# Latent attention: rotary halves of the queries exchanged between partitions by transfers, in place of products with a second copy of the columns

## What is computed

```python
def apply_rope(x, ang):                       # x: 64 features of a head
    x1, x2 = jnp.split(x, 2, axis=-1)         # two halves of 32
    c, s = jnp.cos(ang), jnp.sin(ang)
    return jnp.concatenate([x1 * c - x2 * s, x2 * c + x1 * s], axis=-1)

def mla_mixer(hn, kv, positions, w_q_a, q_g, w_q_b, w_o):
    k_nope, k_pe, v = kv                      # k_pe: one rotary key for all heads
    cq = rmsnorm(hn @ w_q_a, q_g)             # 384 latent features
    q = (cq @ w_q_b).reshape(B, S, 8, 128 + 64)
    q_nope, q_pe = q[..., :128], apply_rope(q[..., 128:], angles)
    o = attention(q_nope, q_pe, k_nope, k_pe, v)   # masked softmax of the sum of both products
    return o.reshape(B, S, 1024) @ w_o
```

## Time and profile before

| | us |
|---|---|
| median of 3 runs | 977.38 |
| lowest, highest | 976.89, 977.48 |
| the profiled execution | 976.76 |
| its span, first to last instruction | 974.8 |
| TensorE busy in it | 958.3 (98%) |
| VectorE, ScalarE, GpSimd busy | 663.8 (68%), 500.6 (51%), 33.2 (3%) |

### The profile page before, as it was taken

One profiled execution on the slowest core, in us unless ns is written; L12 is line 12 of the kernel. 1 busy time (PEld: TensorE's weight loads), 2 busy tenths in 40 slices (PEclk: granted clock), 3 DMA queues, 4 the chain that ended last, 5 costly groups with the idle time before them and its releaser, 6 DMA issues.

```text
span 974.8 us, 15160 instructions
## 1 busy us (share of the span) xinstructions
PE 958.3 (98%) x6065; PEld 862.4 (88%) x6065; DVE 663.8 (68%) x838; ACT 500.6 (51%) x664; POOL 33.2 (3%) x48
## 2 busy tenths in 40 slices
PE   8999999999999998999999999999999999999997
PEld 8999998999999996899998888888899888888885
DVE  5866757687677777677658765666767676655564
ACT  5855663664554557443346434444655464443442
POOL 2000001200000000000000000001010000000000
PEclk9999999999999999999999999999999999999999
DMA  9942212566565544655555565655464446565641
GB/s 294 262 130 87 87 65 88 167 208 210 174 212 172 194 153 140 208 170 173 173 173 186 183 207 179 209 172 195 124 158 173 128 134 235 173 201 187 203 142 44
DMA packets 124799, 165.05 MB, mean 169 GB/s; under 512 B 20910, under 2 KB 103275, under 8 KB 124619
## 3 DMA queue, kind: packets, MB, share of 16 engines
q1 hardware_dynamic: 123131, 159.31, 50.6%
q0 software_dynamic: 1312, 4.68, 1.6%
q10 hardware_dynamic: 304, 0.33, 0.1%
HBM read 163.26 MB, written 1.05 MB: 169 GB/s over the span
## 4 chain that ended last, share of the span: by engine, by line
PE 95%; DVE 2%; ACT 1%; issue 1%; DMA 0%; POOL 0%; POOLq 0%; DVEq 0%; ACTq 0%
PE ps L276 23%; PE ps L278 22%; PE ps L277 22%; PE ps L900 11%; PE ps L897 6%; PE ps L2036 2%; PE ps L1415 2%; PE ps L1436 1%; PE ps L2031 1%; PE ps L1299 1%; PE ps L538 1%; DVE w_lo L239 0%; PE ps L1425 0%; PE ps L2165 0%; DMA X<-in_x_dram 0%
## 5 line engine op out<-in xcount | busy, mean ns | idle before, releaser
L239 DVE TENSOR_TENSOR w_lo<-raw,w_hi 128x2048 fp32r<-128x2048 f32 x147 | 334.3, 2276 | 135.8 <-ACT w_hi L225 135.8
L225 ACT ACTIVATE w_hi<-raw 128x2048 fp32r<-128x2048 f32 x147 | 279.8, 1905 | 141.0 <-PE ps L278 139.5
L276 PE MATMUL ps<-hT,w_hi 128*128 128x256 f32 x712 | 203.7, 286 | 1.4 <-DVE hT L497 0.9
L277 PE MATMUL ps<-hT,w_lo 128*128 128x256 f32 x712 | 201.4, 283 | 0.0
L278 PE MATMUL ps<-hT,w_hi 128*128 128x256 f32 x712 | 201.4, 283 | 0.0
L276 PE MATMUL ps<-w_hi,act_hi 128*128 128x512 f32 x416 | 163.0, 392 | 0.0
L277 PE MATMUL ps<-w_hi,act_lo 128*128 128x512 f32 x416 | 162.0, 389 | 0.0
L278 PE MATMUL ps<-w_lo,act_hi 128*128 128x512 f32 x416 | 162.0, 389 | 0.0
L900 PE MATMUL ps<-hT,w_hi 128*128 128x512 f32 x480 | 150.8, 395 | 0.0
L276 PEld LDWEIGHTS ps<-hT,w_hi 128*128 128x128 f32 x712 | 136.4, 192 | 2.8 <-issue 1.5
L277 PEld LDWEIGHTS ps<-hT,w_lo 128*128 128x128 f32 x712 | 136.5, 192 | 0.7
(11 more groups left out here) (329 smaller groups left out, 1061.6 us busy)
## 6 DMA issues: line engine op xcount, KB each, us to landing
raw<-in_mlp_w_dram SPq DMA_DIRECT2D x64, 1024.0 KB, 5.2
raw<-in_w_up_dram SPq DMA_DIRECT2D x22, 1024.0 KB, 5.1
raw<-in_a_w_in_dram SPq DMA_DIRECT2D x16, 1024.0 KB, 5.3
raw<-in_w_in_dram SPq DMA_DIRECT2D x11, 1024.0 KB, 6.3
raw<-in_w_down_dram SPq DMA_DIRECT2D x11, 1024.0 KB, 4.9
raw<-in_a_w_out_dram SPq DMA_DIRECT2D x8, 1024.0 KB, 4.8
raw<-in_w_out_dram SPq DMA_DIRECT2D x4, 1024.0 KB, 5.1
raw<-in_b_w_o_dram SPq DMA_DIRECT2D x4, 1024.0 KB, 5.0
```

What stands on the lines that cost most here:

```text
L225: nc.scalar.activation(w_hi[:, s, 0:n], raw[:, r, 0:n], ACT.Copy).then_inc(hi_ready, 1)
L239: nc.vector.tensor_tensor(w_lo[:, s, 0:n], raw[:, r, 0:n], w_hi[:, s, 0:n].bitcast(F32), ALU.subtract).then_inc(lo_ready, 1)
L276: nc.tensor.matmul(o, a[0], b[0], start=start, stop=False, skip_group_check=shared)
L277: nc.tensor.matmul(o, a[1], b[0], start=False, stop=False, skip_group_check=shared)
```

## The change

The second copy of the rotary columns goes. A query unit has 384 columns for each tile and `queries_pe` 27 matmuls. The rotary features of the two heads are laid out as first halves of head a, first halves of head b, second halves of head a, second halves of head b (32 each), so partner features stand 64 partitions apart. VectorE multiplies the one rotary product by the cosine and by the sine (`turned_parts`). SyncE then copies the sine product from partitions 64 to 127 to 0 to 63 of `qpe`, and from 0 to 63 to 64 to 127: two DMAs of 64 x 256 elements, 64 KB each (`swap_halves`). VectorE waits for both and adds (`turned_sum`). The tables of signs and of the key's selection follow the new layout, and the key is copied into `kpe` by four copies of 32 partitions in place of two of 64. The order on ScalarE and TensorE around pair 3 changes. Four semaphores of the start are merged into two, with the same instructions in the same order.

```diff
 def q_heads(g):
     c = g * 384
-    unit(cols(q_b, c, P, 0, 512), cols(q_b, c + 192, P, P, 512),
-         cols(q_b, c + 128, ROPE, 256, 512), cols(q_b, c + 320, ROPE, 320, 512),
-         cols(q_b, c + 160, 32, 384, 512), cols(q_b, c + 128, 32, 416, 512),
-         cols(q_b, c + 352, 32, 448, 512), cols(q_b, c + 320, 32, 480, 512))
+    unit(cols(q_b, c, P, 0, 384), cols(q_b, c + 192, P, P, 384),
+         cols(q_b, c + 128, 32, 256, 384), cols(q_b, c + 320, 32, 288, 384),
+         cols(q_b, c + 160, 32, 320, 384), cols(q_b, c + 352, 32, 352, 384))
...
+def swap_halves(sp, g):
+    sp.wait_ge(m_rp, 2 * g + 2)
+    b = ropet[:, 2 * (g % 2) + 1, :]
+    sp.dma_start(qpe[0:P // 2, g, :], b[P // 2:P, :]).then_inc(m_sw, 16)
+    sp.dma_start(qpe[P // 2:P, g, :], b[0:P // 2, :]).then_inc(m_sw, 16)
+
+def mla_sync(sp):
+    u0 = first_unit["mla"]
+    for u in range(u0, last_unit["mla"] + 1):
+        load(sp, u)
+        for g, k in ((0, 9), (1, 10), (2, 12), (3, 12)):
+            if u == u0 + k:
+                swap_halves(sp, g)
...
 def queries_pe(g, u):
-    features(b1[:, 0:S], w, slice(256, 384), cqT, 3)
-    features(b1[:, S:2 * S], w, slice(384, 512), cqT, 3).then_inc(unit_used, 1)
+    features(b1[:, 0:S], w, slice(256, 384), cqT, 3).then_inc(unit_used, 1)
...
 def mla_pe(pe, n, gs):
     queries_pe(2, u0 + 7)
-    at_turn(pe, gs[0])
     pe.wait_ge(lo_ready, u0 + 9)
     pe.wait_ge(m_vev, 4)
     queries_pe(3, u0 + 8)
+    at_turn(pe, gs[0])
     at_out(pe, gs[0])
...
 def mla_act(act, n, gs):
-    nc.scalar.copy(kpe[0:ROPE, 0, :], W[1][0:ROPE, 0:S])
-    nc.scalar.copy(kpe[ROPE:P, 1, :], W[1][ROPE:P, 0:S])
+    for r in (0, ROPE):
+        for h in range(2):
+            rr = slice(r + 32 * h, r + 32 * h + 32)
+            nc.scalar.copy(kpe[rr, h, :], W[1][rr, 0:S])
     split_hi(act, u0 + 6)
...
     at_exp(act, gs[1])
+    queries(2)
+    queries(3)
     at_copy(act, gs[0])
-    queries(2)
-    split_hi(act, u0 + 10)
-    queries(3)
     at_hi(act, gs[0])
     at_copy(act, gs[1])
+    split_hi(act, u0 + 10)
     split_hi(act, u0 + 11)
...
 def mla_dve(dve, n, gs):
-    def rope(g):
+    def turned_parts(g):
         ...
         nc.vector.tensor_tensor(a, bank[:, 0:S], cosT, ALU.mult).then_inc(m_rp, 1)
-        nc.vector.tensor_tensor(b, bank[:, S:2 * S], sinT, ALU.mult).then_inc(m_rp, 1)
+        nc.vector.tensor_tensor(b, bank[:, 0:S], sinT, ALU.mult).then_inc(m_rp, 1)
+
+    def turned_sum(g):
         dve.wait_ge(m_rp, 2 * g + 2)
-        nc.vector.tensor_tensor(qpe[:, g, :], a, b, ALU.add).then_inc(m_rq, 1)
+        dve.wait_ge(m_sw, 32 * g + 32)
+        nc.vector.tensor_tensor(qpe[:, g, :], ropet[:, 2 * (g % 2), :], qpe[:, g, :], ALU.add).then_inc(m_rq, 1)
...
-    nc.vector.memset(kpe[ROPE:P, 0, :], 0.0)
-    nc.vector.memset(kpe[0:ROPE, 1, :], 0.0)
+    nc.vector.memset(kpe, 0.0)
...
     split_lo(dve, u0 + 6)
-    rope(0)
+    turned_parts(0)
     split_lo(dve, u0 + 7)
-    rope(1)
+    turned_sum(0)
+    turned_parts(1)
+    turned_sum(1)
     split_lo(dve, u0 + 8)
...
     at_norm(dve, gs[0])
-    rope(2)
+    turned_parts(2)
     at_norm(dve, gs[1])
-    rope(3)
+    turned_sum(2)
+    turned_parts(3)
     at_lo(dve, gs[0])
+    turned_sum(3)
     split_lo(dve, u0 + 10)
```

More of the change, by code:

```diff
@@ L301, in build @@
         id_in = sem("id_in")
-        g_in, g_tr, g_ok = sem("g_in"), sem("g_tr"), sem("g_ok")
+        g_in = sem("g_in")
         filled = sem("filled")
@@ L343, in start_pe @@
             pe.wait_ge(par_in, 16 * 10)
-            pe.wait_ge(g_ok, 1)
+            pe.wait_ge(par_ok, 1)
             pe.transpose(W[3][:, 0:109], pstage[0:109, 0, :], ident[0:109, 0:109])
@@ L352, in gain_pe @@
             pe.wait_ge(g_in, 16)
-            pe.transpose(W[3][:, 0:KT], pstage[0:KT, 0, :], ident[0:KT, 0:KT]).then_inc(g_tr, 1)
+            pe.transpose(W[3][:, 0:KT], pstage[0:KT, 0, :], ident[0:KT, 0:KT]).then_inc(par_tr, 1)
         def gain_act(act):
-            act.wait_ge(g_tr, 1)
-            nc.scalar.copy(par[:, 0:KT], W[3][:, 0:KT]).then_inc(g_ok, 1)
+            act.wait_ge(par_tr, 1)
+            nc.scalar.copy(par[:, 0:KT], W[3][:, 0:KT]).then_inc(par_ok, 1)
         def start_act(act):
-            act.wait_ge(par_tr, 1)
+            act.wait_ge(par_tr, 2)
             nc.scalar.copy(par[:, KT:NPAR], W[3][:, KT:NPAR]).then_inc(par_ok, 1)
-            act.wait_ge(par_ok, 1)
+            act.wait_ge(par_ok, 2)
         def warm(pe, n, x=ident[:]):
@@ L411, in start_norm_dve @@
             half_split_lo(dve, 0, 0)
-            dve.wait_ge(g_ok, 1)
+            dve.wait_ge(par_ok, 1)
             norm_lo(dve, 0, gain, tiles=range(0, 4))
@@ L476, in norm_hi @@
             if n == 0:
-                act.wait_ge(g_ok, 1)
+                act.wait_ge(par_ok, 1)
             elif n == 1:
-                act.wait_ge(par_ok, 1)
+                act.wait_ge(par_ok, 2)
             for t in range(KT):
@@ L1531, in build @@
         m_kev, m_vev, m_qn, m_rp, m_rq = sem("m_kev"), sem("m_vev"), sem("m_qn"), sem("m_rp"), sem("m_rq")
+        m_sw = sem("m_sw")
         posi = ropet[:, 0, :].bitcast(I32)
+        def swap_halves(sp, g):
[10 more added lines that the diff above has]
+                        swap_halves(sp, g)
         KEY_BANKS = ((ACC[0], ACC[1]), (ACC[2], W[0]))
@@ L2045, in mix_pe @@
             unit_in(ZB)
-            pe.wait_ge(par_ok, 1)
+            pe.wait_ge(par_ok, 2)
             for tb in range(TB):
@@ L2681, in _ @@
                     ffn_sync(sp, passes[st])
+                elif st == "mla":
+                    mla_sync(sp)
                 elif st.startswith("mlp"):
@@ L2832, in constants @@
     t[:, T_INV] = np.float32(10000.0) ** (-(2 * f).astype(np.float32) / np.float32(ROPE))
-    t[:, T_SGN] = np.where(np.arange(P) // (ROPE // 2) % 2 == 0, -1.0, 1.0)
-    t[:, T_SEL:T_SEL + P] = i[:, None] % ROPE == i[None, :] % ROPE
+    t[:, T_SGN] = np.where(np.arange(P) < ROPE, 1.0, -1.0)
+    of = i // ROPE * (ROPE // 2) + i % (ROPE // 2)
+    t[:, T_SEL:T_SEL + P] = (i[:, None] % ROPE == of[None, :]) * np.where(i < ROPE + ROPE // 2, 1.0, -1.0)[:, None]
     slopes = 2.0 ** (-8.0 * np.arange(1, 2 * NH + 1) / (2 * NH))
```

## The result

The changed kernel takes 984.12 us (983.12 to 985.73), the kernel before on the same chips 977.41: ratio 1.0071, 95% interval 1.0060 to 1.0081. It is 6.7 us slower. The sign was forecast, the size was not: 980.9 with a range to 984.0.

What follows compares the result with a forecast made beforehand. TensorE, 95% of the span, was taken to bound the kernel. Matmuls -4.32, first stall +3.85, copy +0.9 and second stall +3.05 gave +3.5 us: 980.3 profiled, 980.9 median, range 978.3 to 984.0.

Steps and rivals of the forecast that it cites:

- TensorE's saving: Query products: each of four pairs loses 9 matmuls of 0.12 us, 1.08 us a pair, 4.32 us in all.
- The cover of the key's copies: VectorE's low half of u0 + 6 ends at 731.0, TensorE wants it at 731.48: 0.5 us of cover, which holds.
- The two places of the waits: TensorE stalls 3.85 us before the first scores, for sum 1, and 3.05 before the scores of `gs[2]`, for sum 3.
- The exposed copy: ScalarE's copy of 0.6 us with two hops, between the first group's turn and `at_out(gs[0])`, costs TensorE 0.9 us.
- A trip: One exchange from products to sum: landing 2.2 us, two issues 0.4 apart, two hops 0.1; 2.7 us, all counted.
- A landing with nothing beside it: A 64 KB transfer inside the chip's memory, from issue to landing: 2.2 us, between 1.3 and 3.1.
- the clock: Rival, chance 0.15: TensorE's clock falls to half in a stall, costing 1.8 us: 982.7 for one, 984.5 for two.
- two falls: TensorE's clock falling to half at both stalls, 1.8 us for one; 984.5 us for two.
- the load term: Exchange 0 queues behind the 1 MB load of u0 + 9, which lands after 5.0 us; it lands 0.5 later, at 736.5.
- the second wait: TensorE before the scores of `gs[2]`, waiting for VectorE's sum 3: 3.05 us.
- no queueing: Rival, chance 0.2: exchange 0 passes the load on SyncE's queue, everything after it comes 2.05 us earlier: 978.8.
- The first wait: TensorE before the first scores, ready at 737.1 and waiting for VectorE's sum 1 until 740.95: 3.85 us.

Runs made afterwards that it cites:

- the short filler: The changed kernel with thrown-away 128x128 matmuls on TensorE, 22 before the wait for sum 1 and 8 before that for sum 3: 981.1 us.
- the run without exchanges: The changed kernel without its eight transfers, VectorE adding the sine product as it stands, so the output is not the reference's: 975.0 us.
- The run on ScalarE's queue with one load: The changed kernel with exchanges 0 and 1 issued by ScalarE in its own queue and the load of u0 + 10 held until exchange 0 landed: 987.76 us.
- the old order's run: The changed kernel with TensorE's and ScalarE's order around pairs 2 and 3 as before the change, the first group's turn between the two products: 984.21 us.
- exchanges ahead: The changed kernel with SyncE issuing exchanges 0 and 1 before the load of u0 + 9 instead of behind it and the load of u0 + 10: 982.34 us.
- extra pair of transfers: The kernel with exchanges 0 and 1 before the load of u0 + 9, plus two more transfers of the same shape before them: 982.63 us.
- products first: The kernel with exchanges 0 and 1 before the load of u0 + 9, and VectorE making pair 1's products before waiting for sum 0: 979.43 us.
- the two runs on ScalarE's queue: The changed kernel with exchanges 0 and 1 issued by ScalarE in its own queue: 985.13 us; with the load of u0 + 10 also held back: 987.76 us.

## Why the prediction was off

**What held.** TensorE's saving: 12.43 for 14.44 and the same for the other two pairs, 4.1 us of the 4.32 counted. The cover of the key's copies: the low half of u0 + 6 ended in time and TensorE did not wait at the keys. The two places of the waits, what each stands behind, and that sum 1 and sum 3 are the last to come. The exposed copy, 0.73 for 0.9. A trip, 2.7 us: exchange 1 held VectorE for 2.68. A landing with nothing beside it is 1.9 to 2.1, under my 2.2, which the longer issues (0.50 to 0.58 from one to the next, I had 0.4) made good.

**What failed: the clock.** I had it as a rival with 0.15, and put only one fall, and part of another, into the range. It fell behind both waits, in the profiled execution by the windows above, and the 3.0 us that the short filler won show the price; two falls were priced at 3.6 together and cost 3.0. The reason I gave against it, that no stall of before was long enough to show one, was no evidence against it, only a lack of evidence. It should have been the forecast for a stall of 3.85. Forecast plus both falls was 984.5 in my own text. So the rival had the right mechanism and nearly the right price, and the forecast's sum had nothing for it. That 984.5 lies so near the measured 984.1 is in part luck: the load term was 1.5 too small as well, and the second wait 0.9 too long.

**What failed: the term of the load.** I let exchange 0 land at 736.5, half a microsecond behind the load's 5.0. It landed at 738.6, or 738.1 by the clock of before. The load ahead of it took 6.5 instead of 5.0, and the exchange was 0.6 behind that. Some 0.7 of these 1.5 have nothing to do with the exchange: in the run without exchanges the same load landed after 5.7.

```profile
raw<-in_b_w_o_dram SPq DMA_DIRECT2D x1, 1024.0 KB, 5.7
```

Where the other 0.8 comes from is not shown. The first wait was 5.38 and not 3.85, so this term was 1.5 too small. And the mechanism was wrong in name: the piece that landed 0.75 behind a load looks the same whether the queue orders them or the engines are shared. The run on ScalarE's queue with one load parts the two. The rival "no queueing" thus fell too: even in another queue the small transfer does not pass the load.

**What made up for part.** The second wait was 2.12, forecast 3.05. From the first scores on TensorE came to this wait 1.6 us later than I had reckoned, 1.4 of it by the half clock. VectorE's chain to sum 3 came only 0.7 later, though it too stood 1.2 us for the slowed scores:

```profile
746.67 0.75 DVE L1447 SCALAR_TENSOR_TENSOR act_tmp<-ps,union 128x512 f32<-128x512 f32 x1 [1.20 <-PE ps L1414]
```

A stall that is bound elsewhere swallows a delay in front of it; the old order's run shows the same.

By terms: forecast +3.5; load term +1.5; copy -0.2; second wait -0.9; half clock in the scores +1.4, behind the second wait +1.7; saving and turn 0.5 smaller; the late entry 0.5. That gives +8.0, the balance of the profiled executions. The medians are 6.7 apart. Half of the missing 1.3 is the late entry, which by their clock most executions of before have too. The other half is that the profiled execution of the changed kernel, with a mean clock of 0.992, is 0.65 over its median: the three executions with 0.994 or 0.995 took 983.1 to 983.5, the three with 0.991 or 0.992 984.8 to 985.7.

## What to carry to other kernels

Before a wait is added in front of TensorE, price the wait, and then the half-clock stretch behind it: here 7.5 us of waits for the sums brought 3.0 more. Work that is thrown away won those 3.0 back. When TensorE's work is replaced by a transfer, issue the transfer with no large load in flight, put independent work of the waiting engine between issue and use, and reorder the engines that feed TensorE's new, earlier schedule: with the same transfers the kernel took 984.1 us in one order and 974.7 in another.

## What the runs showed of the hardware

- The granted clock fell to 0.50 in or behind TensorE waits of 5.38 and 2.12 us (changed kernel), of 2.39 and 2.57 (exchanges ahead), of 2.24 and 2.13 (extra pair of transfers) and of 2.06 (products first), and at the first waits of 5.0 to 7.3 in the old order and on ScalarE's queue. It did not fall at 2.25 in the old order, at 1.57 and 1.42 in the two runs on ScalarE's queue, nor at 0.73 and 0.95 in the run without exchanges. So between 2.06 and 2.4 us these runs have both.
- A fall cost 1.4 to 1.7 us in the changed kernel. It cost 2.4 to 2.6 in the first scores of the old order and of the two runs on ScalarE's queue, where the clock stayed at 0.50 through all of them (7.4 to 7.6 us in place of 5.05).
- It can also fall in an old stall. In the changed kernel's profile it was 0.57 from 370 to 374 us, behind a wait of 2.4 that both kernels have the earlier trace rows; in the profiled execution of before it stayed full there. Executions of before with a mean clock of 0.998 take 976.3 to 976.8, those with 0.995 to 0.997 977.0 to 978.6. That fits the 0.6 us between the profiled execution and the median, and the late entry of 0.5 us into the stretch:

```profile
370.00:374.00 4.00, 3.26 (x9) 2.61 (x10) 3.14 (x8) 1.09 (x5) 0.54 (x1) 0.57 0.00 0
```

- The second half of an exchange (64 KB between partitions) landed after 1.9 to 2.1 us alone, 2.7 to 2.9 at the moment of exchange 0 with no load in flight, 4.6 to 5.8 with a 1 MB load ahead of it, in its own queue or the other one, and 7.5 with two loads in the other queue. The load ahead of exchange 0 took 6.0 to 6.5, and 5.7 without exchanges.
- A copy of 32 partitions took as long on ScalarE as one of 64: four in 1.49 us, 0.37 each.
